# Attention steps on even or fourth ticks in a three-layer network

## The reference

```python
logits = jnp.einsum('bqhcd,bkhcd->bhcqk', qblk, k).astype(jnp.float32) * scale
logits = logits + bias[None, :, None]
p = jax.nn.softmax(logits, axis=-1)
attn = p[:, :, 0] - lam * p[:, :, 1]
```

```python
merged = (gates[:, :, 0] * (y_conv @ w_branch[l, 0])
          + gates[:, :, 1] * (y_fox @ w_branch[l, 1])
          + gates[:, :, 2] * (y_swa @ w_branch[l, 2]))
x = x + merged @ w_mix_out[l]
```

## Time and profile before

| | us |
|---|---|
| median of three executions | 2444.68 |
| profiled execution | 2445.11 |
| its span, first to last instruction | 2443.3 |
| TensorE busy | 2412.1 |
| VectorE busy | 1367.6 |
| ScalarE busy | 1004.5 |
| GpSimd busy | 403.0 |

### The profile page before, as it was taken

The page is one execution under the profiler, slowest core; times in us unless marked ns, Lnnn a source line. Parts: engine busy times, 40 slices in busy tenths (PEclk is TensorE's granted clock), DMA queues, the critical chain, the costliest instruction groups (busy, mean ns, idle before and its releaser), DMA issues.

```text
span 2443.3 us, 30351 instructions
## 1 busy us (share of the span) xinstructions
PE 2412.1 (99%) x11930; PEld 1959.0 (80%) x11930; DVE 1367.6 (56%) x2158; ACT 1004.5 (41%) x1723; POOL 403.0 (16%) x320
## 2 busy tenths in 40 slices
PE   8899999999999999999999999999999999999998
PEld 6677877888888887788888877787788887888887
DVE  6868875763665455576456547534555445443342
ACT  5554553442444444454234334323443334332223
POOL 0342342210112222131001100001220001110011
PEclk9999999999999999999999999999999999999999
DMA  4542222223223221133332232231244322223222
GB/s 161 107 92 78 79 69 96 95 87 112 95 83 116 70 70 48 45 122 96 91 101 92 90 121 82 76 102 57 65 126 134 113 95 87 95 87 104 99 82 87
DMA packets 74269, 226.23 MB, mean 93 GB/s; under 512 B 8080, under 2 KB 12304, under 8 KB 74000
## 3 DMA queue, kind: packets, MB, share of 16 engines
q1 hardware_dynamic: 69696, 215.90, 27.5%
q10 hardware_dynamic: 4432, 8.39, 2.0%
HBM read 215.87 MB, written 8.39 MB: 92 GB/s over the span
## 4 chain that ended last, share of the span: by engine, by line
PE 59%; issue 0%; DVE 0%; ACT 0%; POOL 0%; POOLq 0%; DVEq 0%
PE bank L1142 58%; PE bank L1146 1%; ACT t L1536 0%; DVE t L1986 0%; DVE t L1993 0%; DVE t L1989 0%; ACT t L1539 0%; POOL t L2547 0%; POOLq L2768 0%; DVEq L2768 0%; DVE t L2469 0%; DVE t L2475 0%; POOLq L765 0%
## 5 line engine op out<-in xcount | busy, mean ns | idle before, releaser
L1142 PE MATMUL bank<-t 128*128 128x512 f32 (+4 forms) x11412 | 2381.7, 374 | 21.1 <-DVE t L1986 10.2
L1142 PEld LDWEIGHTS bank<-t 128*128 128x128 f32 (+1 forms) x11412 | 1903.7, 185 | 458.0 <-issue 91.1
L1536 ACT ACTIVATE t<-t 128x1024 fp32r<-128x1024 f32 (+5 forms) x649 | 549.6, 856 | 680.2 <-PE bank L1142 275.6
L1986 DVE TENSOR_TENSOR t<-t 128x1024 fp32r<-128x1024 f32 (+6 forms) x686 | 627.6, 925 | 252.3 <-ACT t L1536 247.3
L2547 POOL TENSOR_TENSOR t<-t 128x512 f32<-128x512 f32 (+5 forms) x240 | 362.4, 1516 | 1641.1 <-ACT t L1539 541.9
L1986 DVE TENSOR_TENSOR t<-bank,t 128x512 f32<-128x512 f32 (+4 forms) x410 | 275.4, 676 | 494.8 <-PE bank L1142 476.9
L1539 ACT ACTIVATE t<-t 128x512 f32<-128x512 f32 (+5 forms) x545 | 330.7, 616 | 522.3 <-DVE t L1986 330.0
L1989 DVE SCALAR_TENSOR_TENSOR t<-t 128x512 f32<-128x512 f32 (+6 forms) x430 | 319.5, 749 | 94.4 <-ACT t L1539 53.9
L1536 ACT ACTIVATE t<-bank 128x512 f32<-128x512 f32 (+4 forms) x150 | 71.5, 493 | 129.2 <-PE bank L1146 89.4
L2550 POOL TENSOR_SCALAR t<-t 128x128 f32<-128x128 f32 (+3 forms) x64 | 40.0, 630 | 387.5 <-ACT t L1536 252.7
L1146 PE MATMUL bank<-t 128*128 128x128 f32 x518 | 81.3, 274 | 2.1 <-ACT t L1536 1.0
(11 more groups left out here) (25 smaller groups left out, 48.5 us busy)
## 6 DMA issues: line engine op xcount, KB each, us to landing
t<-in_w SPq DMA_DIRECT2D x304, 512.0 KB, 3.4
t<-in_w SPq DMA_DIRECT2D x48, 384.0 KB, 3.0
t<-in_w SPq DMA_DIRECT2D x56, 320.0 KB, 2.9
t<-in_w SPq DMA_DIRECT2D x28, 256.0 KB, 3.1
tab<-t ACTq DMA_DIRECT2D x1, 2560.0 KB
t<-in_x SPq DMA_DIRECT2D x8, 256.0 KB, 5.0
t<-tab SPq DMA_DIRECT2D x8, 256.0 KB, 3.8
spill<-t ACTq DMA_DIRECT2D x1, 2048.0 KB, 8.4
```

The lines of the kernel that those rows point to most:

```text
L1142: return eng.matmul(out, lhs, rhs, start=start, stop=stop, skip_group_check=loose)
L1536: return eng.activation(out, in_, ACT.Copy, scale=scale)
L1986: return eng.tensor_tensor(out, a, b, o)
```

## The change

Steps of attention move to other ticks; none is added or left out.

- `once` gets a `step`: differential heads and cross-attention heads start on even ticks only, and head norms too.
- The row of a head norm comes 6 ticks after the sums, the scaling 7, and the head may start after 8.
- Window attention's transposes move from age 4i + 6 to 4i + 8 and its product from 4i + 8 to 4i + 12; full attention's transposes from 4i + 8 to 4i + 10, its product from 4i + 10 to 4i + 14. All steps of a tile now fall on every fourth tick. What reads their outputs moves by 4 ticks.
- Both halves of cross attention's product stand at age 14, and what follows comes one tick earlier.

```diff
     def rms(self, key, g=1):
-        n = 4 if g == 1 else 5
+        n = 4 if g == 1 else 6
...
-            if self.when(name, key) is None and test() and self.place(windows):
+            if self.T % step == 0 and self.when(name, key) is None and test() and self.place(windows):
                 self.start(name, key)
...
-            while want and want[0][1] <= self.T and all(self.T >= t + 3 for t in done[-3:-2]) and self.rms(want[0][0], 2):
+            while want and self.T % 2 == 0 and want[0][1] <= self.T and all(self.T >= t + 3 for t in done[-3:-2]) and self.rms(want[0][0], 2):
...
-        def normed(key, age=7):
+        def normed(key, age=8):
...
-                      and self.tok_begun.get(("v", h // 2), 1 << 30) <= self.T, windows)
+                      and self.tok_begun.get(("v", h // 2), 1 << 30) <= self.T, windows, 2)
...
-                windows += [(("sqk", tile, i, 0), 4 * i, 2), (("sqk", tile, i, 1), 4 * i, 2), (("sat", tile, i), 4 * i + 6, 2)]
-            windows += [(("so", tile), 8, 15)]
+                windows += [(("sqk", tile, i, 0), 4 * i, 2), (("sqk", tile, i, 1), 4 * i, 2), (("sat", tile, i), 4 * i + 8, 2)]
+            windows += [(("so", tile), 12, 15)]
...
-                    windows += [(("fqk", tile, i, half), 4 * i + 2, 2), (("fat", tile, i, half), 4 * i + 8, 2)]
-            windows += [(("fo", tile), 10, 15)]
+                    windows += [(("fqk", tile, i, half), 4 * i + 2, 2), (("fat", tile, i, half), 4 * i + 10, 2)]
+            windows += [(("fo", tile), 14, 15)]
...
-                    self.lo["sw", tile] = self.T + 22
+                    self.lo["sw", tile] = self.T + 26
                 if self.when("fox", tile) == self.T:
-                    self.lo["fo", tile] = self.T + 24
+                    self.lo["fo", tile] = self.T + 28
...
-            windows += [(("xo_", h, 0), 15, 3), (("xo_", h, 1), 16, 3)]
+            windows += [(("xo_", h, 0), 14, 3), (("xo_", h, 1), 14, 4)]
...
-                      and (h == 0 or self.past("xh", h - 1, 8)), windows)
+                      and (h == 0 or self.past("xh", h - 1, 8)), windows, 2)
...
-            for tile in at("swa", T - 4 * i - 6):
+            for tile in at("swa", T - 4 * i - 8):
...
-            for tile in at("swa", T - 4 * i - 8):
+            for tile in at("swa", T - 4 * i - 12):
```

More of the change, by code:

```diff
@@ L338, in norm_rule, with once @@
         self.rules.append(rule)
-    def once(self, name, key, test, windows=()):
+    def once(self, name, key, test, windows=(), step=1):
         def rule():
-            if self.when(name, key) is None and test() and self.place(windows):
+            if self.T % step == 0 and self.when(name, key) is None and test() and self.place(windows):
                 self.start(name, key)
@@ L568, in mix @@
                 for half in range(2):
-                    windows += [(("fqk", tile, i, half), 4 * i + 2, 2), (("fat", tile, i, half), 4 * i + 8, 2)]
-            windows += [(("fo", tile), 10, 15)]
+                    windows += [(("fqk", tile, i, half), 4 * i + 2, 2), (("fat", tile, i, half), 4 * i + 10, 2)]
+            windows += [(("fo", tile), 14, 15)]
             self.once("fox", tile, lambda tile=tile: all(self.ev.get(k, 1 << 30) < self.T for k in
                                                          (("fk", tile), ("fq", tile), ("fv", tile // 2)))
-                      and (self.past("swa", 3, 22) if tile == 0 else self.past("fox", tile - 1, 16)), windows)
+                      and (self.past("swa", 3, 26) if tile == 0 else self.past("fox", tile - 1, 16)), windows)
             def lo(tile=tile):
                 if self.when("swa", tile) == self.T:
-                    self.lo["sw", tile] = self.T + 22
+                    self.lo["sw", tile] = self.T + 26
                 if self.when("fox", tile) == self.T:
-                    self.lo["fo", tile] = self.T + 24
+                    self.lo["fo", tile] = self.T + 28
             self.rules.append(lo)
@@ L614, in mix @@
             branch(0, c, "cv")
-        self.until(lambda: self.past("swa", 3, 22), "swa")
+        self.until(lambda: self.past("swa", 3, 26), "swa")
         for i in range(2):
@@ L625, in mix @@
             branch(2, c, "sw")
-        self.until(lambda: self.past("fox", 3, 24), "fox")
+        self.until(lambda: self.past("fox", 3, 28), "fox")
         self.start("mem", 0)
@@ L656, in cross @@
                 windows += [(("xqk", h, i), 2 * i, 3), (("xat", h, i), 2 * i + 6, 2)]
[L657 removed]
+            windows += [(("xo_", h, 0), 14, 3), (("xo_", h, 1), 14, 4)]
             self.once("xh", h, lambda h=h: all(self.ev.get(k, 1 << 30) < self.T for k in
                                                (("xq", h, 1), ("xk", 2 * h + 1), ("xv", h)))
[L660 removed]
+                      and (h == 0 or self.past("xh", h - 1, 8)), windows, 2)
             def lo(h=h):
                 if self.when("xh", h) == self.T:
[L664 to L665 removed]
+                    self.lo["ox", 2 * h] = self.T + 16
+                    self.lo["ox", 2 * h + 1] = self.T + 17
             self.rules.append(lo)
@@ L1416, in mix @@
                         *fill(("fqk", tile, i, half)))
-            for tile in at("fox", T - 4 * i - 8):
+            for tile in at("fox", T - 4 * i - 10):
                 for half in range(2):
@@ L1424, in mix @@
                     t.then_inc(*fill(("fat", tile, i, half)))
-            for tile in at("fox", T - 4 * i - 10):
+            for tile in at("fox", T - 4 * i - 14):
                 bank = take(("fo", tile)) if i == 0 else K.of(("fo", tile))
@@ L1457, in cross @@
         for d in range(2):
-            for h in at("xh", T - 15 - d):
+            for h in at("xh", T - 14):
                 bank = take(("xo_", h, d))
@@ L1514, in tensor_program @@
                 rms_row(key, 1)
-        for key in at("rms2", T - 5):
+        for key in at("rms2", T - 6):
             rms_row(key, 2)
@@ L1820, in mix @@
                         *sig["ex"].up("s", tile, i, half))
-            for tile in at("swa", T - 4 * i - 7):
+            for tile in at("swa", T - 4 * i - 9):
                 L = buf.Lm[(4 * tile + i) % 5]
@@ L1825, in mix @@
                 copy(two(L[:, :]), two(K.of(("sat", tile, i))[:, :])).then_inc(*leave(("sat", tile, i)))
-        for tile in at("swa", T - 21):
+        for tile in at("swa", T - 25):
             hi, _ = buf.operand("sw", tile)
@@ L1845, in mix @@
                         *sig["ex"].up("f", tile, i, half))
-            for tile in at("fox", T - 4 * i - 9):
+            for tile in at("fox", T - 4 * i - 11):
                 for half in range(2):
@@ L1850, in mix @@
                     copy(L[:, 0:n], K.of(("fat", tile, i, half))[:, 0:n]).then_inc(*leave(("fat", tile, i, half)))
-        for tile in at("fox", T - 23):
+        for tile in at("fox", T - 27):
             hi, _ = buf.operand("fo", tile)
@@ L1909, in cross @@
         for d in range(2):
-            for h in at("xh", T - 16 - d):
+            for h in at("xh", T - 15 - d):
                 hi, _ = buf.operand("ox", 2 * h + d)
@@ L2282, in diff @@
             ts(buf.l4[:, 5:6], buf.l4[:, 4:5], LAM_INIT, ADD).then_inc(*sig["lam"].up())
-        for key in at("rms2", T - 6):
+        for key in at("rms2", T - 7):
             dst = K.head_dst(key)
@@ L2389, in mix @@
                     ts(L[:, a], L[:, a], s8[:, 5:6], MUL).then_inc(*sig["pn"].up("s", tile, i, half))
-        for tile in at("swa", T - 22):
+        for tile in at("swa", T - 26):
             two_parts("sw", tile, K.of(("so", tile))[:, :]).then_inc(*leave(("so", tile)))
@@ L2413, in mix @@
                     ts(L[:, 0:n], L[:, 0:n], s8[:, 5:6], MUL).then_inc(*sig["pn"].up("f", tile, i, half))
-        for tile in at("fox", T - 24):
+        for tile in at("fox", T - 28):
             two_parts("fo", tile, K.of(("fo", tile))[:, :]).then_inc(*leave(("fo", tile)))
@@ L2478, in cross @@
         for d in range(2):
-            for h in at("xh", T - 17 - d):
+            for h in at("xh", T - 16 - d):
                 two_parts("ox", 2 * h + d, K.of(("xo_", h, d))[:, :]).then_inc(*leave(("xo_", h, d)))
```

2 lines of the change are left out of this document (removed).

## The result

| | median us | lowest to highest | runs |
|---|---|---|---|
| before | 2444.68 | 2444.25 to 2448.4 | 6 |
| with the change | 2436.51 | 2434.98 to 2439.49 | 6 |

The ratio is 0.9966, with a 95% interval of 0.9956 to 0.9975: 8.2 us faster, and more than the 0.2% that can be told from no change. The forecast, 2438.5 with a range of 2433.5 to 2445.5, held. Two of its terms were wrong by nearly 3 us each, and their errors have opposite signs; the sum hides that, the trace does not.

The account below looks back on a forecast made before the run. TensorE, busy in 99% of the 2443.3 us span, was taken as the bound. The terms -3.3 - 0.5 - 1.0 - 1.3 - 1.75 - 0.8 + 2.5 = -6.15 us on 2445.11 gave 2439.0, median 2438.5, range 2433.5 to 2445.5.

Parts of the forecast that it names:

- Parity in differential attention: Differential attention: logits reductions on even ticks no longer stand behind VectorE's evacuations; -3.3 us, and -0.5 for smaller ones.
- The last head: End of differential attention: the 1.00 us wait of the `ao` projection for head 7's output is hidden; -1.0 us, bound 0.
- rival 1: The waits reappear as VectorE backlog; if the first block's gain (4.8) is given back, 2443.3 us; chance 20%.
- Three norms in tick 516: Differential attention: three head norms share a tick, ScalarE's square of k1 is about covered; 0 us, bounds 0 and 0.7.
- Parted neighbours in the mixer: Mixer: transposes now part QK^T and product, 28 half-array neighbours become 18; +2.5 us, bounds 2 and 3.
- Mixer waits: Mixer, full attention: hidden waits in groups of transposes are covered with 8 ticks after QK^T; -1.3 us.
- Interruptions: 278 groups of attention or norm steps between projection matmuls become 224, 0.02 us each; -0.8 us, bounds 0 to 1.6.
- Cross attention: Cross attention: the waits of 1.03 and 0.72 us go, with heads off odd ticks and the product's second half earlier; -1.75 us.
- 2 (VectorE's gathered ticks stall TensorE): Gathering makes VectorE's odd ticks the bottleneck, +13.4 us if each stalls, 2452 us; chance 9%.
- 3 (all parted pairs free and all bounds full, 2434.7): Parted pairs cost nothing, interruptions and hidden waits reach their full bounds; 2434.7 us; chance 13%.
- 4: The change doesn't do what it says, heads stay on odd ticks; excluded by the order, no chance given.

Follow-up runs that it names:

- D: The changed kernel with differential heads and head norms gathered on odd ticks instead of even ones; 2446.02 us, ratio 1.0006.
- F: The changed kernel with at most two head norms to a tick, so the third of tick 516 goes to 518; 2434.25 us, ratio 0.9956.
- J: The changed kernel with its third head norm of tick 516 in tick 518, once more; 2434.66 us, ratio 0.9961.
- L: The changed kernel with the third norm in tick 518 and the mixer's transposes issued first; 2434.21 us, ratio 0.9962.
- I: The kernel before with one line of the change alone, head norms starting in even ticks only; 2454.79 us, ratio 1.0039.
- C: The kernel before with the cross-attention part alone: heads on even ticks, both product halves at age 14; 2442.24 us, ratio 0.9992.
- G: The changed kernel with the mixer's transposes issued ahead of QK^T and product within a tick; 2434.87 us, ratio 0.9955.
- K: The changed kernel itself, run a third time as a yardstick; 2437.14 us, ratio 0.9968.
- B: The kernel before with the mixer's new ages alone; 2444.10 us, ratio 0.9998.

## Why the prediction was right, and where it was not

Three terms can be sized by a count of single starts in the traces. A stretch holds the same projection matmuls before and after (in the mixer 1278 of 512 columns and 192 of 256), at 0.2267 and 0.1133 us each when nothing is between. The rest of a stretch is the time of the other groups, and the time by which the projection matmuls just behind a group come later than that pace.

**Parity in differential attention, -3.3 and -0.5.** Right in mechanism, shown by D: the waits go on even ticks and return on odd ones. With the last head's -1.0 and a share of the interruptions the prediction had some 5.1 us in this stretch; at full clock it is 6.2 (F, J, L). 3.5 of them are the three waits in brackets (1.67, 0.81, 1.00), 1.0 is lost time of projection matmuls behind groups. The other 1.7 stood inside groups, as the 0.50 and 0.33 did, where the prediction took 1.3; they were not followed place by place.

**The last head, -1.0.** Right: its wait is gone, and nothing was given back behind it. In the output projection only the 0.55 us on issue is left, 0.53 before, and the unchanged stretch behind is equal to 0.01 us; VectorE's 2.24 us a column (rival 1) did not collect it.

**Three norms in tick 516: "I take 0, bounds 0 and 0.7".** This is the step that failed. It looked for a wait of ScalarE's square and found it covered, which it was. What came was no wait but a lower clock, 2.9 us, outside the bound. F, J and L take it away by moving one norm, I puts it into the kernel before.

**Parted neighbours in the mixer, +2.5.** Mis-sized. The price itself was read nearly right for a QK^T and a product with projections between: they cost 833 + 794 ns apart and 1420 side by side, 0.21 us. The prediction's estimate from the Trainium skill, "TensorE: Matmul & The Clock Gate", Parts 2 and 3, was 0.21 for a parting too, and the trace agrees. But 8 of the 10 pairs were parted by transposes, which costs 0.15, and transposes beside a product give 0.05 back in 16 places. The prediction named that second effect ("if transposes beside a half-array product also save something, 0") and still took 2.5. In all, the other groups of the mixer take 1.1 us less than before although 2.3 us of waits are gone from them: some +1.2 for the neighbours. Window attention came out even (28.83 and 28.77 a period), full attention 1.8 shorter in three periods.

**Mixer waits, -1.3.** Right in kind, too small. Four transposes take 0.65 and two 0.38 us, as foretold to 0.05. But two groups of QK^T, mask and product in full attention also held hidden waits: they cost 1966 and 2119 ns where a third equal one costs 1646, and with the change equal groups agree to 3 ns but for one. All together the hidden waits were 2.3 us more than now.

**Interruptions, -0.8.** Too small. The ten projection matmuls behind a group each lose up to 7 ns, about 0.03 us in all. The mixer has 46 such groups instead of 73 and wins 0.8 us by it, differential attention 54 instead of 76 and wins 1.0. Cross attention has as many as before.

**Cross attention, -1.75.** Measured -2.30, and -2.33 in C. The two waits went. The other 0.55 are not interruptions, as their number is the same; what they are was not found.

**The sum.** In the mixer the terms (-1.3, +2.5 and some -0.3 of the interruptions) give +0.9, and -1.91 was measured: too dear by 2.8, from all three. It was too cheap by 2.9 for the clock. 1.1 more in differential attention at full clock, some 0.4 in cross attention and 0.2 ahead of the first mark are what is left, the 1.7 us by which 2439.0 is above the profiled 2437.33. The forecast came near by luck: two errors of nearly 3 us cancelled.

**Rivals.** 1 (waits reappear behind): refuted; the 4.8 us that it calls the first block's are those of differential attention. 2 (VectorE's gathered ticks stall TensorE): refuted, since no wait of over 0.5 us stands at a gathered tick. D shows that on the other ticks the same gathering gains nothing, and I that a part of it can cost 10 us. 3 (all parted pairs free and all bounds full, 2434.7) described the mixer better than the forecast did, though the parted pairs were not free. 4: excluded by the order.

## What to carry to other kernels

When an engine evacuates in order on a fixed beat, try the steps it does for others on the off-beat, and move all of them that hang together; a part alone can cost more than the whole gains. After a reordering, read the granted clock over the moved place as well as the waits: here a gathered run of thin matmuls took back 2.9 of 6.2 us. Price a neighbourhood from the same sequence in a trace, with what it may give back, not from differences of long groups.

## What the runs showed of the hardware

- TensorE's granted clock fell to its lower level inside a stretch in which TensorE was busy in full, at the end of 24 matmuls of 128x2. In four of the six traces that have them in one tick it fell 0.5 to 0.8 us before the last one started and stayed low for 6.8 us; in the other two (G, K) it fell about 1 us after that start, for 3.4 us. The matmuls of 128x512 between 795 and 801.8 us, before and then with the change (busy us, mean ns):

```profile
L1142 PE MATMUL bank<-t 128*128 128x512 f32 x12 | 3.0, 397 | 0.0
```

```profile
L1142 PE MATMUL bank<-t 128*128 128x512 f32 x12 | 5.5, 640 | 0.0
```

  The Trainium skill, "TensorE: Matmul & The Clock Gate", Part 1, describes such losses by idle gaps, with TensorE waiting for data or between groups; here no gap in the trace goes ahead of it. Before, as many thin matmuls stand between 786 and 795.5 us (23 in both traces), but in two ticks, and the clock stays. What exactly about the run matters is open.
- Smaller runs have a fall in some executions only. 20 matmuls of 128x8 at the forget gate are in all 14 traces and have one in 4 (B, D, G, K). With the change 8 of 128x1 and 8 of 128x2 also come together at about 950 us, which before are 2.1 us apart: in 3 of the 10 traces that have them together (D, G, K) a fall follows, and in none of the 4 others. So the change brought a second place of risk, worth 1.6 us, that F does not mend.
- Falls behind a wait are there too, in the kernel before as well. It has two, at 72.0 and 389.5 us, each of 3.4 us, 1.7 us after the end of a wait of 2.99 us and 0.4 us after one of 1.97. The first by timeline and by windows:

```profile
70.31 4.45 PE L1142 MATMUL bank<-t 32*8 32x64 f32 x14 [2.99 <-DVE t L1986]
```

```profile
72.00:75.40 3.40, 3.40 (x12) 0.50 0.53 66
```

- Inside the program every stretch at half clock was about 3.4 or 6.8 us long (at its very end the low clock shows for 7 to 10 us). In differential attention they cost about 1.6 and 2.9 us: 272.29 and 272.31 with two short ones, 271.98 to 272.00 with a long one, against 269.1 with none.
- They do not come at the same places in each execution. All programs issue the same up to the first head norms, just behind the first mark, yet the first mark lies between 783.30 and 788.46 us: in the trace with 783.30 one short fall stands ahead of it, in that with 788.46 three. The runs of one kernel differ by 2 to 8 us; much of that can come from the falls, which only the profiled execution shows. One such execution may show a stage 1.5 us longer that is not so in the next.
